# Who weighs and adds a third of the gathered rows: VectorE in one pass, or ScalarE and GpSimd in two

## The reference, cut to what matters

```python
def expert_block(args):
    xt, e, g = args
    act = jax.nn.gelu(jnp.einsum('td,tkd->tk', xt, jnp.take(u_tab, e, axis=0)), approximate=False) * g
    return jnp.einsum('tk,tkd->td', act, jnp.take(v_tab, e, axis=0))
```

## Time and profile before

| | |
|---|---|
| median of three runs | 3223.79 us |
| the profiled execution | 3224.62 us |
| its span | 3222.8 us |
| TensorE, VectorE, ScalarE, GpSimd busy | 79%, 66%, 23%, 37% |
| HBM traffic | 1066 MB read, 332 GB/s over the span |

### The profile page before, as it was taken

The page is one execution under the profiler, slowest core; times in us unless marked ns, Lnnn a source line. Parts: engine busy times, 40 slices in busy tenths (PEclk is TensorE's granted clock), DMA queues, the critical chain, the costliest instruction groups (busy, mean ns, idle before and its releaser), DMA issues.

```text
span 3222.8 us, 29606 instructions
## 1 busy us (share of the span) xinstructions
PE 2543.0 (79%) x8924; PEld 1451.3 (45%) x8924; DVE 2114.5 (66%) x5266; ACT 733.3 (23%) x1871; POOL 1185.8 (37%) x1028
## 2 busy tenths in 40 slices
PE   7898876988777788867788777979898777776666
PEld 3585633757453222345545323556565423232223
DVE  4533588887779972244445954677757799966665
ACT  1121112551112221133211211144411122211111
POOL 0000165555444431211122434465445344444442
PEclk9889887989989989988899998988899899989888
DMA  8756497978889999986889986988788799999996
GB/s 334 294 190 215 157 368 294 329 290 337 307 326 361 393 389 353 363 317 248 323 343 385 397 351 236 368 318 318 273 320 307 273 418 424 409 408 417 425 425 289
DMA packets 222493, 1070.97 MB, mean 332 GB/s; under 512 B 25345, under 2 KB 28161, under 8 KB 156033
## 3 DMA queue, kind: packets, MB, share of 16 engines
q0 software_dynamic: 147456, 805.37, 64.2%
q1 hardware_dynamic: 71712, 253.16, 21.0%
q10 hardware_dynamic: 3168, 10.55, 0.8%
HBM read 1065.67 MB, written 3.31 MB: 332 GB/s over the span
## 4 chain that ended last, share of the span: by engine, by line
PE 44%; DVE 23%; DMA 15%; issue 11%; ACT 4%; POOL 2%; ACTq 0%; DVEq 0%; SPq 0%; another core or an unknown queue 0%; POOLq 0%
PE psum L777 13%; DMA ring<-in_peer_uv,experts 7%; PE psum L867 6%; DMA work<-in_peer_uv,experts 6%; PE psum L856 6%; PE psum L1026 5%; DVE ring L1292 4%; PE psum L818 4%; PE psum L1008 3%; DMA ring<-in_peer_u,experts 2%; POOL ring L1747 2%; PE psum L892 2%; DVE work L1389 2%; DVE work L1292 1%; DVE acc L1314 1%
## 5 line engine op out<-in xcount | busy, mean ns | idle before, releaser
L777 PE MATMUL psum<-ring,wdiag 128*128 128x512 f32 x1240 | 649.5, 669 | 218.2 <-ACT wdiag L1069 189.7
L777 PE MATMUL psum<-work,wdiag 128*128 128x512 f32 x944 | 501.4, 678 | 247.3 <-ACT wdiag L1069 240.6
L1747 POOL DMA_INDIRECT ring<-in_peer_u,experts x256 | 323.7, 1264 | 828.9 <-DVE experts L1536 385.8
L1747 POOL DMA_INDIRECT work<-in_peer_uv,experts x260 | 299.3, 1151 | 633.3 <-PE psum L777 586.3
L777 PEld LDWEIGHTS psum<-ring,wdiag 128*128 128x128 f32 x1240 | 255.9, 215 | 580.7 <-issue 544.3
L1747 POOL DMA_INDIRECT ring<-in_peer_uv,experts x252 | 283.2, 1124 | 418.6 <-PE psum L777 392.3
L777 PEld LDWEIGHTS psum<-work,wdiag 128*128 128x128 f32 x944 | 190.2, 213 | 536.2 <-issue 528.6
L1292 DVE CUSTOM_DVE_ANT_0 work<-work 128x1024 f32<-128x1024 f32 x260 | 314.1, 1223 | 89.5 <-DMA work<-in_peer_uv,experts 86.6
L1292 DVE CUSTOM_DVE_ANT_0 ring<-ring,work 128x1024 f32<-128x1024 f32 x252 | 304.2, 1223 | 102.2 <-DMA ring<-in_peer_uv,experts 100.5
L1292 DVE CUSTOM_DVE_ANT_0 ring<-ring,h2a 128x1024 f32<-128x1024 f32 x256 | 304.6, 1220 | 71.1 <-DMA ring<-in_peer_u,experts 70.0
L1747 POOL DMA_INDIRECT ring<-in_peer_v,experts x256 | 279.4, 1091 | 122.1 <-issue 72.7
(11 more groups left out here) (201 smaller groups left out, 2851.7 us busy)
## 6 DMA issues: line engine op xcount, KB each, us to landing
wring<-in_wpack SPq DMA_DIRECT2D x374, 512.0 KB
ring<-in_wpack SPq DMA_DIRECT2D x94, 512.0 KB, 5.5
work<-in_peer_uv,experts POOLq DMA_INDIRECT x260
work<-in_rows ACTq DMA_DIRECT2D x4, 1024.0 KB
ring<-in_peer_u,experts POOLq DMA_INDIRECT x256
ring<-in_peer_v,experts POOLq DMA_INDIRECT x256
ring<-in_peer_uv,experts POOLq DMA_INDIRECT x252, 10.6
work<-in_rpb ACTq DMA_DIRECT2D x2, 1024.0 KB, 12.9
```

Source lines behind the costliest of these rows:

```text
L777: last = nc.tensor.matmul(psum[:, 6 + q, :], wdiag[:, SUM_NO[e] % SMALL, :], row("v", e)[:, 512 * q:512 * (q + 1)], start=(e % KSEL == 0), ...
L1747: pool.indirect_dma_start(dst, None, table, index).then_inc(got[ROW_SLOT[key]], 16)
```

## The change

In tiles 0 and 3 two experts in three, from the ninth of the tile on, leave both TensorE and VectorE: 80 in each tile. ScalarE multiplies the v row by its weight, in place in the ring, at the point where it would have made the diagonal (step g - 3). GpSimd adds the scaled row to `acc`, in its own loop: before it asks for the u row of expert e, it adds the rows of the experts up to e - 10 (`SUM_BEHIND` = 9). VectorE takes no sums in these two tiles. `LATENT_SHARE` goes away, and with it the exception for sums that fall on a latent stage's pieces: tile 2 gets 8 more sums on VectorE (18, not 10) where its last steps lie at the beginning of stage 3. In tiles 1, 4 and 5 nothing changes (13, 8 and 30 on VectorE). TensorE's sums: 48 for 52 in tile 0, 48 for 43 in tile 3, 110 for 118 in tile 2.

```diff
-        n, of = LATENT_SHARE.get(x[0], (0, 1)) if x[1] in LATENT else (0, 1) if x[0] in ("topk", "norms", "ln1") else (1, 4)
+        n, of = (2, 3) if e // KSEL in TIGHT else (0, 1) if x[0] in ("topk", "norms", "ln1") else (1, 4)
...
                     for p in DIAG_IN[g]:
                         act.wait_ge(wts_ready, p + 1)
                         for e in STEP_EXPERTS[p]:
-                            if by_vector(e):
+                            if in_acc(e):
+                                if e // KSEL in TIGHT:
+                                    key = rows_of_sum(e)
+                                    act.wait_ge(got[ROW_SLOT[key]], 16 * ROW_USE[key])
+                                    nc.scalar.activation(row("v", e), row("v", e), ACT.Identity, scale=wts[:, e % SMALL:e % SMALL + 1])\
+                                        .then_inc(rows_scaled, 1)
                                 continue
...
                 def expert_step(g):
-                    for e in [e for p in SUM_IN[g] for e in STEP_EXPERTS[p] if by_vector(e)]:
+                    for e in [e for p in SUM_IN[g] for e in STEP_EXPERTS[p] if in_acc(e) and e // KSEL not in TIGHT]:
                         add_row(e)
...
             def _(pool):
                 pool.wait_ge(setup_loaded, 16 * 7)
+                sums = [e for e in range(ALL_EXPERTS) if in_acc(e) and e // KSEL in TIGHT]
+                summed = [0]
+
+                def add_row(e):
+                    n = e // KSEL
+                    pool.wait_ge(rows_scaled, scaled_before(e) + 1)
+                    if SUM_NO[e] == sums_before(KSEL * n, True):
+                        if n:
+                            pool.wait_ge(sums_free, n)
+                        ins = nc.gpsimd.tensor_copy(acc[:, :], row("v", e))
+                    else:
+                        pool.wait_ge(rows_acc, SUM_NO[e])
+                        ins = nc.gpsimd.tensor_tensor(acc[:, :], acc[:, :], row("v", e), ALU.add)
+                    ins.then_inc(rows_acc, 1)
+
+                def add_rows_before(e):
+                    while summed[0] < len(sums) and sums[summed[0]] < e:
+                        add_row(sums[summed[0]])
+                        summed[0] += 1
+
                 def ask(what, e):
                     key = (what, e)
+                    add_rows_before(e - SUM_BEHIND)
                     for was, b in ROW_BEFORE[key]:
+                        if was != "u" and in_acc(b) and b // KSEL in TIGHT:
+                            add_rows_before(b + 1)
                         if was == "u":
                             pool.wait_ge(dots_ready, b + 1)
                         else:
-                            pool.wait_ge(rows_acc if by_vector(b) else rows_added, SUM_NO[b] + 1)
+                            pool.wait_ge(rows_acc if in_acc(b) else rows_added, SUM_NO[b] + 1)
```

More of the change, by code:

```diff
@@ L110 @@
 V_LAG = 6
+SUM_BEHIND = 9
 U_SMALL, V_SMALL = 4, 7
@@ L370, with acc_sums @@
 PROGRAM = program()
-LATENT_SHARE = {"proj": (1, 1), "mix": (1, 1), "pq": (1, 1), "gate": (1, 1), "br": (1, 1), "ps": (1, 1), "h2": (1, 1),
-                "s": (2, 3), "pt": (2, 3), "o": (2, 3), "ot": (2, 3), "tt": (2, 3), "kv": (2, 3), "mqt": (2, 3), "mkt": (2, 3)}
-def vector_sums():
+def acc_sums():
     at, out = schedule(), []
@@ L383, in vector_sums, with in_acc, scaled_before, sums_before @@
         x = WORK[place] if place < len(WORK) else ("end", -1)
-        n, of = LATENT_SHARE.get(x[0], (0, 1)) if x[1] in LATENT else (0, 1) if x[0] in ("topk", "norms", "ln1") else (1, 4)
+        n, of = (2, 3) if e // KSEL in TIGHT else (0, 1) if x[0] in ("topk", "norms", "ln1") else (1, 4)
         out.append(SMALL <= k and (k + 1) * n // of > k * n // of)
     return out
-VECTOR_SUM = vector_sums()
-def by_vector(e):
-    return VECTOR_SUM[e]
+ACC_SUM = acc_sums()
+def in_acc(e):
+    return ACC_SUM[e]
 SUM_NO, _sums = [], {True: 0, False: 0}
 for _e in range(ALL_EXPERTS):
[L399 to L405, removed]
+    SUM_NO.append(_sums[in_acc(_e)])
+    _sums[in_acc(_e)] += 1
+def scaled_before(e):
+    return sum(in_acc(i) and i // KSEL in TIGHT for i in range(e))
+def sums_before(e, added):
+    return sum(in_acc(i) == added for i in range(e))
 XN_NO, _made = {}, 0
@@ L698, in build @@
         got = [sem(f"got{i}") for i in range(RINGS + PACKED)]
-        dots_ready, gelu_ready, wts_ready, diags_made, rows_added, rows_acc = (
-            sem(n) for n in ("dots_ready", "gelu_ready", "wts_ready", "diags_made", "rows_added", "rows_acc"))
+        dots_ready, gelu_ready, wts_ready, diags_made, rows_scaled, rows_added, rows_acc = (
+            sem(n) for n in ("dots_ready", "gelu_ready", "wts_ready", "diags_made", "rows_scaled", "rows_added", "rows_acc"))
         sums_ready, sums_free = sem("sums_ready"), sem("sums_free")
@@ L769, in expert_step @@
                 def expert_step(g):
-                    for e in [e for p in SUM_IN[g] for e in STEP_EXPERTS[p] if not by_vector(e)]:
+                    for e in [e for p in SUM_IN[g] for e in STEP_EXPERTS[p] if not in_acc(e)]:
                         if e % KSEL == 0 and e:
@@ L1299, in expert_step @@
                             dve.wait_ge(diags_made, sums_before(e - SMALL + size, False))
-                        if e >= SMALL and sums_before(e - SMALL + size, True):
+                        if e >= SMALL and scaled_before(e - SMALL + size):
+                            dve.wait_ge(rows_scaled, scaled_before(e - SMALL + size))
+                        if e >= SMALL and sums_before(e - SMALL + size, True) > scaled_before(e - SMALL + size):
                             dve.wait_ge(rows_acc, sums_before(e - SMALL + size, True))
```

## The result

The changed kernel takes 3362.57 us (median of four, 3360.95 to 3369.90); the kernel before, beside it, 3223.89. The ratio is 1.0429, with a 95% interval of 1.0407 to 1.0452: 139 us slower. The forecast was 3269, slower, with a range up to 3350. The direction was right, the loss was three times as large as forecast (139 for 45 us), and the time lies outside the range.

What follows compares the result with a forecast made beforehand. GpSimd's gathers were taken to set the pace in 395:550, TensorE from 550 on. On 3224.6 us, crowding +40, ScalarE +10, TensorE +10 and relief -15 made +45, 3269.6; the runs' median is 0.8 lower, so 3269, range 3187 to 3350.

Steps and rivals of the forecast that it cites:

- GpSimd's add, 2.56 us as the upper end: GpSimd's 128 x 1024 add in tiles 0 and 3: twice VectorE's 1.28 us pass, the end the forecast went by.
- Crowding on GpSimd, +40: GpSimd's adds exceed its free time in crowded stretches of tiles 0 and 3: +40 us (0 to +80).
- Its signs: GpSimd's waits for dots fall well under 349 us; u rows become what VectorE's dots wait for (71 us before).
- ScalarE, 1.05 us a scaling and +10: 80 row scalings a tile at 1.05 us on ScalarE, ahead of evacuations TensorE needs: +10 us (0 to +71).
- TensorE and the split, +10 (0 to +20): More TensorE sums in 550:800, where it leads the chain, from the even split of experts: +10 us (0 to +20).
- The relief, 15 of 34 us: VectorE's running sums removed in tiles 0 and 3: 34 us on the chain, 15 taken as gained.
- Rival 2: VectorE's dots and GpSimd's adds in tiles 0 and 3 can't run at the same time: +76 us, 3345; chance 0.20.
- Rival 1: GpSimd's adds cost near 1.58 us or fit its waits in tiles 0 and 3: faster, 3190 or 3169; chance 0.28.

Runs made afterwards that it cites:

- the four memsets' run: Changed kernel with each GpSimd add replaced by four memsets about as long, reading nothing, sums left out of the output: 3266.9 us, ratio 1.0129.

## Why the forecast was right in direction and wrong in size

- **GpSimd's add, 2.56 us as the upper end: right.** It takes 2.42 us.
- **Crowding on GpSimd, +40: right.** +35 in the four memsets' run. Its signs came out too: waits for dots fell from 165 to 41 us in tile 0's stretch, waits for u rows rose from 70 to 153 us. But they were poor signs. With nobody adding the first is already down to 113 us and the second up to 138, for VectorE has less to do.
- **ScalarE, 1.05 us a scaling and +10: right.** 1.14 us, and 8 us for all of it, not told from nothing.
- **TensorE and the split, +10 (0 to +20): too small with nobody adding, +30; with GpSimd adding 7 us, not told from nothing.** The forecast looked at tile 0 up to 800 us only. In the run in which nobody adds, the two query projections of the latent tiles' expert networks (line 1026 before), which no sum interrupted before, took 61 and 62 us for 55, and the projections of stage 3 shared TensorE with 13 matmuls more.
- **The relief, 15 of 34 us: not measured by itself.** The run with no add on either engine gives 23 us after ScalarE's cost, so the 34 us of the running sum on the chain were a fair measure of what can be won. How much of it is left once GpSimd is crowded, which is what the 15 stood for, no run parts from the crowding.
- **Rival 2, the contention, given 0.20 and put at nothing in the sum: this is the step that failed.** "If an add and a dot can't run at the same time" was the truth, and its 76 us, with the rest of the forecast's sum left as it was, would have given the 3345 written there. In its place the runs show a term of 96 us: 138 with the add, 42 with memsets of its length that read nothing. Its reckoning had 125 us on the dots, and they took 91; it left out the product of the weights (51 us, an instruction of 0.16 us that waits for what is left of an add) and the other instructions, nearly all with two SBUF operands, which share the remaining 207 - 91 - 51 = 65 us. The test named for it was a mean of the dots well above 1.22 us, and it is 1.57.

The forecast had put the contention at nothing since the trace of before couldn't show it. That trace couldn't exclude it either: GpSimd ran nothing in it but gathers and four tiny memsets. The rule of the Trainium skill (SBUF — State Buffer, section "Who interferes with whom") was set beside the sum as a matter of doubt. By that rule, the traces agree on who is in whose way: VectorE's instructions with two SBUF inputs wait to the end of the add, those with an input in PSUM don't, and memsets, which read nothing, leave the dots at 1.22 us. That the later one waits they can't show, since by the records some dots that began up to 0.65 us before an add waited for it.

- **Rival 1, faster: it had no room.** With the adds gone altogether the changed kernel is still at +7, and with the old split at -23.
- **Some luck in the sum.** Without the contention the forecast said +45, and the four memsets' run gives +42. But the parts are others: -23 for relief and scalings where the forecast had -5, +30 for the split where it had +10. The two misses cancel.

None of the versions run here that leave nothing out is faster than the kernel before.

## What to carry to other kernels

Before work moves from VectorE to GpSimd, ask what both read: an add that GpSimd takes over can cost VectorE as much as its own add did (207 / 160 = 1.29 us for each here, against 1.28), because a VectorE instruction with two SBUF operands that meets it, however small, waits until it is through. A mean busy share (37%) says little of an engine whose queue also issues the gathers; the stretch in which they are issued does. And a split that suits one adder should be priced anew on each engine: here it cost 80 us with VectorE adding, 30 with nobody, and nothing that could be told once GpSimd added. Last, a wait that grows is no proof of a cause: the one for u rows had doubled before GpSimd added a single row.

## What the runs showed of the hardware that was not expected

- A VectorE product of 128 x 2 values with both operands in SBUF lasted 2.29 us when it met a GpSimd add; undisturbed it takes 0.155.
- The contention works both ways: GpSimd's add is 2.34 us at the shortest, 2.42 on average and 3.70 at the longest, and its copy of 300 columns lasted 0.73 us on average.
- GpSimd copies 128 x 1024 float32 in 1.03 us and sets them in 0.95, where the add of two operands takes 2.4; by time on its queue a copy or a memset costs less than half of an add.
- Of VectorE's passes with one SBUF input, reductions and the search for maxima ran at full speed during adds, but a copy of 128 x 128 values (0.22 us) lasted up to 3.06 us beside an add and up to 2.88 beside memsets.
